# Sums of squares in the second input projection: one float32 product replaced by two rounded ones

## The chip, the cores and the metric

The kernel runs on one core of a Trainium2 chip. The metric is the device time of one execution in microseconds, the median of several runs.

## The reference, cut to what matters

The program is a two-layer network on 512 tokens of width 1024 (attention, gated feed-forward layers, a short convolution), followed by a second, hybrid mixer. The change lies in the second mixer's differential attention, where queries and keys are normed over 64 features and rotated:

```python
def rms_norm_2(x, w, eps=EPS):
    x = x.astype(jnp.float32)
    return x * lax.rsqrt(jnp.mean(x * x, axis=-1, keepdims=True) + eps) * w.astype(jnp.float32)
...
    proj = jnp.einsum("bsd,de->bse", hn, w_in.astype(f32))
...
    q_b = apply_rope(rms_norm_2(q_b.reshape(b, s, DIFF_HEADS, 2, DIFF_D), q_norm_w), cos, sin)
    k_b = apply_rope(rms_norm_2(k_b.reshape(b, s, DIFF_HEADS, 2, DIFF_D), k_norm_w), cos, sin)
```

`q_b` and `k_b` are 512 features each. In the kernel they are eight chunks of 128 features (two groups of 64) by 512 tokens.

## The kernel before, in words

All dense layers work on weight tiles of 1024 x 128. A tile is loaded as part of a panel of 256 columns (two tiles, 1 MB) by SyncE. ScalarE rounds it to a high part (`split_hi`, line 434), VectorE forms the low part as weights minus high part (`split_lo`, line 441), and TensorE multiplies: for each of eight chunks of the inner dimension three products, high by high, high by low and low by high (`dense_tile`, line 464), into a PSUM pair that alternates between tiles. High and low parts are of the rounded type (float32r). VectorE then evicts the tile, scaled per token.

The second input projection is one such sequence, `T_QB` to `T_OUT2`. Its tiles are numbered from 0 here. Tiles 0 to 7 give q_b and k_b, and tile r is chunk r of them. The order of work is written out by hand, one list per engine, all with one turn per tile:

- TensorE (`in2_pe`, from line 1606): the 24 products of tile t; then, for tiles 1 to 8, the sums of squares of the chunk before (`dif_sums_pe`, line 1903). The sums are a product with `pair`, a 128 x 128 table of ones in two blocks of 64, which gives every feature the sum over its group. It has had two float32 operands, `pair` and `d_sq`.
- ScalarE (`in2_act`, 1635): the high part of the weights of tile t + 2; `dif_raw_act` of chunk t (square, line 1891; copy scaled by the norm's weight, line 1892, which signals `raw`); `dif_scales_act` of chunk t - 1 (Ln and Exp on the sums, lines 1909 and 1910); `dif_hi_act` of chunk t - 2 (line 1926). Before tile 0 it computes the scale per token (lines 478, 479), for which tile 0's eviction waits.
- VectorE (`in2_dve`, 1675): the eviction of tile t (line 1693 for the first eight); the low part of the weights of tile t + 2; `dif_normed_dve` of chunk t - 1 (the swapped copy by the sine, line 1916; the addition, 1919; by the scale, 1922); `dif_lo_dve` of chunk t - 2 (line 1930).
- POOL (`dif_pool`, 1932): three short memsets after `raw` of chunk 0, then per chunk the product of the scaled copy and the cosine (line 1943), as soon as `raw` is there.
- SyncE: for each pair of chunks eight swap DMAs (`dif_swap`, line 1898), four per chunk, which copy quarters of 32 partitions of the scaled copy into each other's place; then the next weight panel (line 425), all through one queue.

In `setup_pool_tables` (2769) POOL copies small tables into rounded types during the start of the program; in the stage ahead of the projection POOL squares and adds the residual (lines 494, 497) and VectorE forms `x_lo` (line 484).

`Signals.wait(engine, name, n)` waits until the named semaphore has been raised n times. In `in2_dve` the turn ends with:

```python
                if 0 <= r - 1 < KC:
                    dif_normed_dve(dve, r - 1)
                if 0 <= r - 2 < KC:
                    dif_lo_dve(dve, r - 2)
```

Of the kernel before, what the change touches and what calls it, by code (L numbers as in the profile page):

```python
# [14 lines left out]
F32 = mybir.dt.float32  # L15
F32R = mybir.dt.float32r
BF16 = mybir.dt.bfloat16
ALU = mybir.AluOpType
ACT = mybir.ActivationFunctionType
# [3 lines left out]
P = 128  # L23
KC = D // P
META = 16
SEQ = 512
# [150 lines left out]
def program(nc, io, out):  # L177

    ctx = ExitStack()
    with ctx:  # L180
# [5 lines left out]
        def at(name, offset, shape, dtype=F32):  # L186
            size = int(np.prod(shape[1:])) * (2 if dtype is BF16 else 4)
            assert base + offset + size <= end, (name, base + offset + size - end)
            place[name] = offset + size
            return nc.alloc_sbuf_tensor_at(name, shape, dtype, offset=base + offset)  # L190
# [3 lines left out]
        def take(name, shape, dtype=F32):  # L194
            size = (int(np.prod(shape[1:])) * (2 if dtype is BF16 else 4) + 31) // 32 * 32
            t = at(name, cursor[0], shape, dtype)
            cursor[0] += size
            return t
# [8 lines left out]
        raw = take("raw", [P, 2, 2304])  # L207
# [3 lines left out]
        tab = {}  # L211
        for n in ("ident", "ones", "pair", "zeros"):
            tab[n] = take("t_" + n, [P, P])
        id_r, neg_r = take("id_r", [P, P], BF16), take("neg_r", [P, P], BF16)
        id_half, tri_half = take("id_half", [P, 2, P], BF16), take("tri_half", [P, 2, P], BF16)
        scale_bc = take("scale_bc", [P, LEN])
# [9 lines left out]
        z = take("z", [P, KC, LEN])  # L226
        lat = take("lat", [P, 6, LEN])
        spare = cursor[0] + 10240
# [3 lines left out]
        q_hi = take("q_hi", [P, 2, 2, LEN], F32R)  # L232
# [21 lines left out]
        ps = ctx.enter_context(nc.psum_tensor("ps", [P, 8, 512], F32))  # L254
# [6 lines left out]
        def sems(prefix, names):  # L261
            return {n: sem(f"{prefix}_{n}") for n in names.split()}
# [3 lines left out]
        s_id, s_tab0 = sem("ident_landed"), sem("first_tables_landed")  # L266
        s_vz = sem("vec_cleared")
# [23 lines left out]
        def col(name, i=0, rows=P, row0=0):  # L291
            c = VEC_ROWS[name][0] + i
            return vec[row0:row0 + rows, c:c + 1]
# [265 lines left out]
        fv = sems("forget", "cleared min ln pos sum hi lo")  # L559
# [973 lines left out]
        def conv_dve(dve):  # L1533
# [22 lines left out]
            with dve.Fori(0, 2) as i:  # L1556
                for j in range(4):
# [23 lines left out]
        d_g, d_sq, d_rs, d_sin, d_cos = [[at(f"{n}{i}", dz_at[2 * m + i], [P, SEQ]) for i in range(2)]  # L1581
                                         for m, n in enumerate(("dif_g", "dif_sq", "dif_rs", "dif_rot_a", "dif_rot_b"))]
        rows = at("rows", off["raw"], [P, 8, SEQ])
        in2 = sems("in2", "sig taps0 taps act mul params lam")

        def qk_a(c):
# [88 lines left out]
        def in2_dve(dve):  # L1675
# [8 lines left out]
            for t in range(T_QB, T_OUT2):  # L1684
# [27 lines left out]
                    dif_normed_dve(dve, r - 1)  # L1712
                if 0 <= r - 2 < KC:
                    dif_lo_dve(dve, r - 2)
                if t == T_Z:
                    dve.wait_ge(s_tab2, 144)
                    dve.tensor_tensor(small[0:64, 31:32], small[0:64, 24:25], small[0:64, 25:26], ALU.mult)
                    dve.tensor_tensor(small[0:64, 32:33], small[0:64, 26:27], small[0:64, 27:28], ALU.mult).then_inc(in2["params"], 1)
# [96 lines left out]
        class Signals:  # L1815
# [7 lines left out]
            def wait(self, eng, what, n):  # L1823
                if n > 0:
# [4 lines left out]
        finished.update({"o_unit": (fx["added"], additions(8)), "o_two": (fx["o_done"], 8), "o_sum": (fx["inv"], 8), "o_one": (fx["meta_out"], 8), "o_sq": (fx["meta_max"], 8),  # L1829
                         "l2_sq": (fx["squares"], KC), "raw": (mq["raw"], 8), "cleared": (mq["cleared"], 11), "rot_a": (mq["sin"], 5),  # L1830
                         "rot_b": (mq["cos"], 5), "rot": (mq["roped"], 5)})
        dz = Signals("dif", "raw sums rot_a rot_b rot scales normed q_hi q_lo full max exp pv out_hi out_lo cleared "
                          "shift o_sum o_one o_two o_sq o_unit o_gated l2_sq l2_inv l2_normed", finished)
        dif_order = dif_ring()
        dif_first = {T_BA - 1: [("s", 0, 3), ("s", 0, 2)], T_BA: [("s", 0, 1), ("s", 0, 0)]}
# [49 lines left out]
        def dif_raw_act(act, n):  # L1885
            act.wait_ge(evicted, T_QB + n + 1)
            dz.wait(act, "sums", n - 1)
            dz.wait(act, "rot_b", n - 1)
            if n >= 2:
                act.wait_ge(s_swap[n % 2], 16 + 64 * (n // 2))  # L1890
            act.activation(d_sq[n % 2][:, :], z[:, n, 0:SEQ], ACT.Square)
            act.activation(d_g[n % 2][:, :], z[:, n, 0:SEQ], ACT.Copy, scale=col("q_norm_w_2" if n < 4 else "k_norm_w_2")).then_inc(dz.s["raw"], 1)

        def dif_swap(eng, n):
            dz.wait(eng, "raw", n + 1)
# [2 lines left out]
                eng.dma_start(d_sin[n % 2][32 * q:32 * q + 32, :], d_g[n % 2][32 * (q ^ 1):32 * (q ^ 1) + 32, :]).then_inc(s_swap[n % 2], 16)  # L1898

        def dif_sums_pe(pe, n):  # L1900
            dz.wait(pe, "raw", n + 1)
            dz.wait(pe, "scales", n - 1)
            pe.matmul(ps[:, 5 + 2 * (n % 2), :], tab["pair"][:, :], d_sq[n % 2][:, :], start=True, stop=True).then_inc(dz.s["sums"], 1)

        def dif_scales_act(act, n):
            dz.wait(act, "sums", n + 1)
# [21 lines left out]
        def dif_lo_dve(dve, n):  # L1928
            dz.wait(dve, "q_hi", n + 1)
            dve.tensor_tensor(fox_lo[:, n, 0:SEQ], z[:, n, 0:SEQ], fox_hi[:, n, 0:SEQ].bitcast(F32), ALU.subtract).then_inc(dz.s["q_lo"], 1)  # L1930
# [836 lines left out]
            pool.memset(v_one[:, :, :, 64:128], 1.0).then_inc(fv["cleared"], 1)  # L2767

        def setup_pool_tables(pool):
            pool.wait_ge(s_tab, 16 * 9)  # L2770
            pool.wait_ge(s_id, 16)
            pool.wait_ge(first_sum, KC - 1)
            pool.tensor_copy(id_r[:, :], tab["ident"][:, :])
            pool.tensor_copy(neg_r[:, :], neg_in[:, :])
            pool.tensor_copy(id_half[:, :, :], id_half_in[:, :, :])
            pool.tensor_copy(tri_half[:, :, :], tri_half_in[:, :, :])
            pool.tensor_copy(sel_r[:, :, :].rearrange("q a b -> q (a b)"), sel_in[:, :]).then_inc(tab_ok, 1)
# [198 lines left out]
```

## Time and profile before

| what | value |
|---|---|
| median of 3 runs | 1674.76 us (1673.95 to 1680.09) |
| the profiled execution: its time | 1672.01 us |
| the profiled execution: span of the trace | 1670.2 us |
| TensorE busy | 1644.2 us, 98% |
| VectorE busy | 875.1 us, 52% |
| ScalarE busy | 625.1 us, 37% |
| POOL busy | 168.8 us, 10% |
| granted TensorE clock | 1.0 throughout |

The span is what the trace covers of one execution; the execution's own time is 1.8 us longer. Busy times add up over stages with different limits. In the profile PE is TensorE, DVE VectorE, ACT ScalarE, SPq the queue of SyncE; "L1903" is a line of the kernel. Products on TensorE are pipelined, so their records overlap: the distance between starts tells what one costs, and the chain of waits counts it that way. The number in brackets behind a timeline row is the engine's idle time before it, with what ended it.

### The profile page before, as it was taken

To read this page: it belongs to the slowest core of one execution; us is meant where nothing else is said; L and a number is where in the kernel's file an instruction comes from. 1 tells how busy PE (TensorE), PEld (TensorE's weight loads), DVE (VectorE), ACT (ScalarE), POOL (GpSimd) and SP (SyncE) were. 2 spreads that over 40 slices of the span, in tenths; PEclk is the share of its full clock that TensorE was granted. 3 is DMA by queue.
4 is the path that set the end of the run, shared out by engine and by line. 5 is a ranking of instruction groups with operands and counts; after the bars stand their busy time and mean duration, and the time that the engine had idled before them with its cause. 6 is when DMAs were issued, how large, how long until landed. Compare 5 with 4: busy or idle time off the path is not lost.

```text
span 1670.2 us, 28296 instructions
## 1 busy us (share of the span) xinstructions
PE 1644.2 (98%) x11935; PEld 1432.8 (86%) x11935; DVE 875.1 (52%) x1124; ACT 625.1 (37%) x954; POOL 168.8 (10%) x142
## 2 busy tenths in 40 slices
PE   8999999999999999999999999999999999989998
PEld 8997777899999999999987888888887788757796
DVE  6544576464343434565656434343466747866644
ACT  5523544333231323321233314132334545576223
POOL 1002213230000000220004000000033100000200
PEclk9999999999999999999999999999999999999999
DMA  6231000132332322323223322332246666101001
GB/s 194 77 83 26 8 25 28 52 102 79 99 102 77 100 83 93 101 76 101 93 83 102 101 81 96 101 100 83 93 117 103 116 89 100 29 1 61 28 27 51
DMA packets 137604, 131.92 MB, mean 79 GB/s; under 512 B 18205, under 2 KB 131860, under 8 KB 137508
## 3 DMA queue, kind: packets, MB, share of 16 engines
q1 hardware_dynamic: 137306, 130.47, 27.9%
q8 instruction: 73, 1.20, 0.3%
q14 instruction: 23, 0.19, 0.0%
q10 hardware_dynamic: 202, 0.06, 0.0%
HBM read 126.33 MB, written 2.10 MB: 77 GB/s over the span
## 4 chain that ended last, share of the span: by engine, by line
PE 94%; DVE 3%; ACT 1%; issue 0%; SPq 0%; DMA 0%; POOL 0%; ACTq 0%; DVEq 0%
PE ps L464 74%; PE ps L2275 2%; PE ps L799 2%; PE ps L782 2%; PE ps L1168 1%; PE ps L909 1%; PE ps L2006 1%; PE ps L807 1%; PE ps L2800 1%; PE ps L2447 1%; PE ps L2426 1%; PE ps L2442 1%; PE ps L1976 1%; PE ps L1174 0%; PE ps L1211 0%; PE ps L815 0%
## 5 line engine op out<-in xcount | busy, mean ns | idle before, releaser
L434 ACT ACTIVATE w_hi<-raw 128x1024 fp32r<-128x1024 f32 (+1 forms) x227 | 239.6, 1056 | 794.1 <-PE ps L464 780.1
L464 PE MATMUL ps<-x_hi,w_hi 128*128 128x258 f32 (+4 forms) x1640 | 450.3, 327 | 0.5 <-DVE x_lo L484 0.4
L464 PE MATMUL ps<-x_lo,w_hi 128*128 128x258 f32 (+4 forms) x1640 | 444.0, 323 | 0.0
L464 PE MATMUL ps<-x_hi,w_lo 128*128 128x258 f32 (+4 forms) x1640 | 443.1, 323 | 0.0
L441 DVE TENSOR_TENSOR w_lo<-raw,w_hi 128x1024 fp32r<-128x1024 f32 (+1 forms) x227 | 295.0, 1300 | 95.9 <-ACT w_hi L434 95.9
L464 PEld LDWEIGHTS ps<-x_hi,w_hi 128*128 128x128 f32 (+2 forms) x1640 | 273.1, 188 | 31.5 <-issue 3.3
L464 PEld LDWEIGHTS ps<-x_lo,w_hi 128*128 128x128 f32 (+2 forms) x1640 | 272.1, 187 | 27.6 <-issue 2.4
L464 PEld LDWEIGHTS ps<-x_hi,w_lo 128*128 128x128 f32 (+2 forms) x1640 | 272.0, 188 | 25.6
L464 PE MATMUL ps<-a_hi,w_lo 128*128 128x258 f32 (+1 forms) x960 | 255.2, 320 | 0.0
L464 PE MATMUL ps<-a_hi,w_hi 128*128 128x258 f32 (+1 forms) x960 | 255.0, 320 | 0.0
L464 PE MATMUL ps<-a_lo,w_hi 128*128 128x258 f32 (+1 forms) x960 | 255.0, 320 | 0.0
L464 PEld LDWEIGHTS ps<-a_hi,w_hi 128*128 128x128 f32 x960 | 159.1, 189 | 14.5 <-DVE a_lo L1567 0.2
L464 PEld LDWEIGHTS ps<-a_hi,w_lo 128*128 128x128 f32 x960 | 159.5, 189 | 14.0
L464 PEld LDWEIGHTS ps<-a_lo,w_hi 128*128 128x128 f32 x960 | 159.2, 189 | 14.0
L1416 DVE TENSOR_TENSOR h<-h,ps 128x516 f32<-128x516 f32 (+1 forms) x80 | 55.2, 690 | 196.7 <-PE ps L464 196.7
L1483 DVE SCALAR_TENSOR_TENSOR tmp<-ps,scale_bc 128x516 f32<-128x516 f32 (+1 forms) x64 | 44.4, 693 | 172.5 <-PE ps L464 162.6
L494 POOL TENSOR_TENSOR acc<-h 128x516 f32<-128x516 f32 (+1 forms) x4 | 4.2, 1044 | 791.4 <-DVE h L1416 791.4
L497 POOL TENSOR_TENSOR acc<-acc,sq 128x516 f32<-128x516 f32 (+1 forms) x28 | 60.4, 2155 | 2.2
L484 DVE SCALAR_TENSOR_TENSOR x_lo<-h,vec,x_hi 128x516 fp32r<-128x516 f32 (+2 forms) x40 | 58.4, 1474 | 0.1
L1488 DVE TENSOR_TENSOR a_lo<-tmp,a_hi 128x516 fp32r<-128x516 f32 (+1 forms) x64 | 44.4, 694 | 1.0 <-ACT a_hi L1465 0.5
L1465 ACT ACTIVATE a_hi<-tmp 128x516 fp32r<-128x516 f32 (+1 forms) x64 | 40.6, 635 | 2.0
L1463 ACT ACTIVATE tmp<-tmp 128x516 f32<-128x516 f32 (+1 forms) x64 | 39.5, 617 | 1.9 <-DVE tmp L1483 1.9
(441 smaller groups left out, 1781.1 us busy)
## 6 DMA issues: line engine op xcount, KB each, us to landing
raw<-in_w_mlp_up SPq DMA_DIRECT2D x32, 1024.0 KB, 5.3
raw<-in_w_mlp_down SPq DMA_DIRECT2D x32, 1024.0 KB, 4.8
raw<-in_w_in SPq DMA_DIRECT2D x16, 1024.0 KB, 9.0
raw<-in_w_in_conv SPq DMA_DIRECT2D x12, 1024.0 KB, 5.1
raw<-in_w_in_attn SPq DMA_DIRECT2D x8, 1024.0 KB, 5.1
raw<-in_w_out_attn SPq DMA_DIRECT2D x4, 1024.0 KB, 5.9
raw<-in_w_out_conv SPq DMA_DIRECT2D x4, 1024.0 KB, 4.8
raw<-in_w_out SPq DMA_DIRECT2D x4, 1024.0 KB, 5.2
```

The lines of the kernel that those rows point to most:

```text
L434: act.activation(split_tile(w_hi, t), raw_tile(t), ACT.Copy).then_inc(w_hi_ok, 1)
L441: dve.tensor_tensor(lo, raw_tile(t), hi.bitcast(F32), ALU.subtract).then_inc(w_lo_ok, 1)
L464: ins = pe.matmul(tile_banks(t)[0:m, b, 0:c], w[:, k, :], x[:, k, x0:x0 + c], start=(k == order[0] and n == 0), stop=(k == order[-1] and n ...
L484: dve.scalar_tensor_tensor(x_lo[:, c, f:], h[:, c, f:], col(*nm.gain(c)), x_hi[:, c, f:].bitcast(F32), ALU.mult, ALU.subtract).then_inc(x_ ...
L497: pool.tensor_tensor(acc[:, f:], acc[:, f:], sq[:, f:], ALU.add).then_inc(acc_ok, 1)
L782: ins = pe.matmul(slot[0:nq, x, c0:c0 + nk], q, k, start=(n == 0), stop=(n == last))
L799: ins = pe.matmul(slot[0:nk, x, c0:c0 + nq], k, q, start=(n == 0), stop=(n == last))
L1416: dve.tensor_tensor(like(dst, width), like(dst, width), in_psum(pair_of_banks[t % 2], width), ALU.add).then_inc(evicted, 1)
L1463: act.activation(tmp[:, j % 2, 0:nm.width], tmp[:, j % 2, 0:nm.width], ACT.Square).then_inc(relu_sq, 1)
L1465: act.activation(a_hi[:, j, 0:nm.width], tmp[:, j % 2, 0:nm.width], ACT.Copy).then_inc(a_hi_ok, 1)
L1483: dve.scalar_tensor_tensor(like(tmp[:, j % 2, 0:w], w), in_psum(pair_of_banks[(t0 + j) % 2], w), 0.0, like(scale_bc[:, f:], w), ALU.max, A ...
L1488: dve.tensor_tensor(a_lo[:, j, 0:w], tmp[:, j % 2, 0:w], a_hi[:, j, 0:w].bitcast(F32), ALU.subtract).then_inc(a_lo_ok, 1)
```

## The change

The sums of squares are computed from rounded operands. `pair` is copied once into a rounded table `pair_r` by POOL during setup. For every chunk ScalarE writes the square twice, in float32 (`d_sq`) and rounded (`d_sqh`); VectorE forms the difference as the low part (`d_sql`, in the place of `d_sq`), at the end of its turn for the tile; TensorE waits for the low part and adds two products, `pair_r` by high and `pair_r` by low, in one PSUM bank. ScalarE's scaled copy, which raises `raw`, comes ahead of the squares.

```diff
--- before.py
+++ after.py
@@ -211,6 +211,7 @@
         tab = {}
         for n in ("ident", "ones", "pair", "zeros"):
             tab[n] = take("t_" + n, [P, P])
+        pair_r = take("pair_r", [P, P], F32R)
         id_r, neg_r = take("id_r", [P, P], BF16), take("neg_r", [P, P], BF16)
         id_half, tri_half = take("id_half", [P, 2, P], BF16), take("tri_half", [P, 2, P], BF16)
         scale_bc = take("scale_bc", [P, LEN])
@@ -1581,6 +1582,8 @@
         d_g, d_sq, d_rs, d_sin, d_cos = [[at(f"{n}{i}", dz_at[2 * m + i], [P, SEQ]) for i in range(2)]
                                          for m, n in enumerate(("dif_g", "dif_sq", "dif_rs", "dif_rot_a", "dif_rot_b"))]
         rows = at("rows", off["raw"], [P, 8, SEQ])
+        d_sqh = at("dif_sq_hi", spare, [P, 2, SEQ], F32R)
+        d_sql = [at(f"dif_sq_lo{i}", dz_at[2 + i], [P, SEQ], F32R) for i in range(2)]
         in2 = sems("in2", "sig taps0 taps act mul params lam")
 
         def qk_a(c):
@@ -1712,6 +1715,8 @@
                     dif_normed_dve(dve, r - 1)
                 if 0 <= r - 2 < KC:
                     dif_lo_dve(dve, r - 2)
+                if r < KC:
+                    dif_squares_dve(dve, r)
                 if t == T_Z:
                     dve.wait_ge(s_tab2, 144)
                     dve.tensor_tensor(small[0:64, 31:32], small[0:64, 24:25], small[0:64, 25:26], ALU.mult)
@@ -1829,7 +1834,8 @@
         finished.update({"o_unit": (fx["added"], additions(8)), "o_two": (fx["o_done"], 8), "o_sum": (fx["inv"], 8), "o_one": (fx["meta_out"], 8), "o_sq": (fx["meta_max"], 8),
                          "l2_sq": (fx["squares"], KC), "raw": (mq["raw"], 8), "cleared": (mq["cleared"], 11), "rot_a": (mq["sin"], 5),
                          "rot_b": (mq["cos"], 5), "rot": (mq["roped"], 5)})
-        dz = Signals("dif", "raw sums rot_a rot_b rot scales normed q_hi q_lo full max exp pv out_hi out_lo cleared "
+        finished.update({"sq_hi": (s_tab0, 48), "sq_lo": (s_vz, 1)})
+        dz = Signals("dif", "raw sq_hi sq_lo sums rot_a rot_b rot scales normed q_hi q_lo full max exp pv out_hi out_lo cleared "
                           "shift o_sum o_one o_two o_sq o_unit o_gated l2_sq l2_inv l2_normed", finished)
         dif_order = dif_ring()
         dif_first = {T_BA - 1: [("s", 0, 3), ("s", 0, 2)], T_BA: [("s", 0, 1), ("s", 0, 0)]}
@@ -1888,8 +1894,13 @@
             dz.wait(act, "rot_b", n - 1)
             if n >= 2:
                 act.wait_ge(s_swap[n % 2], 16 + 64 * (n // 2))
+            act.activation(d_g[n % 2][:, :], z[:, n, 0:SEQ], ACT.Copy, scale=col("q_norm_w_2" if n < 4 else "k_norm_w_2")).then_inc(dz.s["raw"], 1)
             act.activation(d_sq[n % 2][:, :], z[:, n, 0:SEQ], ACT.Square)
-            act.activation(d_g[n % 2][:, :], z[:, n, 0:SEQ], ACT.Copy, scale=col("q_norm_w_2" if n < 4 else "k_norm_w_2")).then_inc(dz.s["raw"], 1)
+            act.activation(d_sqh[:, n % 2, :], z[:, n, 0:SEQ], ACT.Square).then_inc(dz.s["sq_hi"], 1)
+
+        def dif_squares_dve(dve, n):
+            dz.wait(dve, "sq_hi", n + 1)
+            dve.tensor_tensor(d_sql[n % 2][:, :], d_sq[n % 2][:, :], d_sqh[:, n % 2, :].bitcast(F32), ALU.subtract).then_inc(dz.s["sq_lo"], 1)
 
         def dif_swap(eng, n):
             dz.wait(eng, "raw", n + 1)
@@ -1898,9 +1909,12 @@
                 eng.dma_start(d_sin[n % 2][32 * q:32 * q + 32, :], d_g[n % 2][32 * (q ^ 1):32 * (q ^ 1) + 32, :]).then_inc(s_swap[n % 2], 16)
 
         def dif_sums_pe(pe, n):
-            dz.wait(pe, "raw", n + 1)
+            dz.wait(pe, "sq_lo", n + 1)
             dz.wait(pe, "scales", n - 1)
-            pe.matmul(ps[:, 5 + 2 * (n % 2), :], tab["pair"][:, :], d_sq[n % 2][:, :], start=True, stop=True).then_inc(dz.s["sums"], 1)
+            if n == 0:
+                pe.wait_ge(fv["cleared"], 5)
+            pe.matmul(ps[:, 5 + 2 * (n % 2), :], pair_r[:, :], d_sqh[:, n % 2, :], start=True, stop=False)
+            pe.matmul(ps[:, 5 + 2 * (n % 2), :], pair_r[:, :], d_sql[n % 2][:, :], start=False, stop=True).then_inc(dz.s["sums"], 1)
 
         def dif_scales_act(act, n):
             dz.wait(act, "sums", n + 1)
@@ -2767,6 +2781,8 @@
             pool.memset(v_one[:, :, :, 64:128], 1.0).then_inc(fv["cleared"], 1)
 
         def setup_pool_tables(pool):
+            pool.wait_ge(s_tab0, 48)
+            pool.tensor_copy(pair_r[:, :], tab["pair"][:, :]).then_inc(fv["cleared"], 1)
             pool.wait_ge(s_tab, 16 * 9)
             pool.wait_ge(s_id, 16)
             pool.wait_ge(first_sum, KC - 1)
```

## Rows read from the trace of the kernel before

**Rows 1.** The page's head, busy times and the chain that ended last, by engine.

```profile
span 1670.2 us, 28296 instructions
...
PE 1644.2 (98%) x11935; PEld 1432.8 (86%) x11935; DVE 875.1 (52%) x1124; ACT 625.1 (37%) x954; POOL 168.8 (10%) x142
...
PE 94%; DVE 3%; ACT 1%; issue 0%; SPq 0%; DMA 0%; POOL 0%; ACTq 0%; DVEq 0%
```

**Rows 2.** Chain that ended last, in order of time: start us, us, what.

```profile
1276.15 0.86 PE ps L1903 x2
1277.01 5.56 PE ps L464 x24
...
1295.41 0.86 PE ps L1903 x2
...
1321.09 0.86 PE ps L1903 x2
```

**Rows 3.** The line of the sums: records x count, ns min/median/max.

```profile
L1903 PE MATMUL ps<-dif_sq,t_pair x16: 592/592/593, 1276.0 to 1321.4; 128*128 128x512 f32 x16
```

**Rows 4.** VectorE's timeline, turn of tile 2: start us, us, instruction, idle before.

```profile
1282.61 0.69 DVE L1693 TENSOR_TENSOR z<-ps,scale_bc 128x512 f32<-128x512 f32 x1 [0.74 <-PE ps L464]
1283.76 1.23 DVE L441 TENSOR_TENSOR w_lo<-raw,w_hi 128x1024 fp32r<-128x1024 f32 x1 [0.46 <-ACT w_hi L434]
1284.90 0.68 DVE L1916 TENSOR_TENSOR dif_rot_a<-dif_rot_a,dif_sin 128x512 f32<-128x512 f32 x1
1285.62 1.67 DVE L1919 TENSOR_TENSOR z<-dif_rot_a,dif_rot_b 128x512 f32<-128x512 f32 x1
1287.33 0.69 DVE L1922 TENSOR_TENSOR z<-z,dif_rs 128x512 f32<-128x512 f32 x1
1287.94 0.68 DVE L1930 TENSOR_TENSOR fox_lo<-z,fox_hi 128x512 fp32r<-128x512 f32 x1
1289.03 0.69 DVE L1693 TENSOR_TENSOR z<-ps,scale_bc 128x512 f32<-128x512 f32 x1 [0.41 <-PE ps L464]
```

**Rows 5.** VectorE's timeline, stage before, turn of tile 3, eviction of tile 4.

```profile
1261.38 1.77 DVE L484 SCALAR_TENSOR_TENSOR x_lo<-h,vec,x_hi 128x512 fp32r<-128x512 f32 x1
...
1294.12 0.69 DVE L1916 TENSOR_TENSOR dif_rot_a<-dif_rot_a,dif_sin 128x512 f32<-128x512 f32 x1 [2.72 <-DMA dif_rot_a<-dif_g]
...
1296.79 0.68 DVE L1693 TENSOR_TENSOR z<-ps,scale_bc 128x512 f32<-128x512 f32 x1
```

**Rows 6.** ScalarE's timeline, chunk 0 and the turn of tile 2.

```profile
1274.13 0.63 ACT L1891 ACTIVATE dif_sq<-z 128x512 f32<-128x512 f32 x1 [0.76 <-DVE z L1693]
1274.67 0.71 ACT L1892 ACTIVATE dif_g<-z,vec 128x512 f32<-128x512 f32 x1
...
1282.67 1.06 ACT L434 ACTIVATE w_hi<-raw 128x1024 fp32r<-128x1024 f32 x1 [2.98 <-PE ps L464]
1283.63 0.62 ACT L1891 ACTIVATE dif_sq<-z 128x512 f32<-128x512 f32 x1
1284.15 0.71 ACT L1892 ACTIVATE dif_g<-z,vec 128x512 f32<-128x512 f32 x1
```

**Rows 7.** POOL's timeline: setup, the stage before, products of chunks 0, 2, 3.

```profile
27.88 0.29 POOL L2773 CAST id_r<-t_ident 128x128 bf16<-128x128 f32 x1 [23.98 <-DVE acc L529]
...
1260.45 2.15 POOL L497 TENSOR_TENSOR acc<-acc,sq 128x512 f32<-128x512 f32 x1
...
1276.35 1.29 POOL L1943 TENSOR_TENSOR dif_rot_b<-dif_g,dif_cos 128x512 f32<-128x512 f32 x1
...
1284.94 1.80 POOL L1943 TENSOR_TENSOR dif_rot_b<-dif_g,dif_cos 128x512 f32<-128x512 f32 x1 [5.08 <-ACT dif_g L1892]
1291.36 1.30 POOL L1943 TENSOR_TENSOR dif_rot_b<-dif_g,dif_cos 128x512 f32<-128x512 f32 x1 [4.62 <-ACT dif_g L1892]
```

**Rows 8.** SyncE's timeline: DMAs issued, merged; x8 is two chunks' swaps.

```profile
1280.98 0.52 SPq L425 DMA_DIRECT2D raw<-in_w_in  x1
1284.89 8.84 SPq L1898 DMA_DIRECT2D dif_rot_a<-dif_g  x8
```

## The prediction

> **What bounds the kernel now.** I read the page's head first: TensorE is busy for 98% of the span and makes 94% of the chain that ended last [rows 1]. A microsecond on TensorE is therefore a microsecond of the kernel, and work elsewhere costs only if TensorE waits for it. Next the chain around the change: each weight tile of the second input projection is 24 products in 5.56 us, which is 0.232 us for a product of 512 columns, and behind each of the first eight tiles after tile 0 stands the sum of squares with 0.86 us, back to back from 1276.15 to 1321.09 [rows 2]. So the period of a tile is 5.56 + 0.86 = 6.42 us, with no wait in it. The 0.86 us is one float32 product, shown as two records of 592 ns that overlap in the pipeline [rows 3].
>
> Then the other engines in one period. I number tiles from the start of this projection (tile 2 is done at 1282.57). VectorE's turn for tile 2 is the eviction, the low part of weights, the three steps of the rotation of chunk 1, and the low part of chunk 0: from 1282.61 to 1287.94 + 0.68 = 1288.62, and the next eviction starts at 1289.03, 0.41 us after it [rows 4]. VectorE is thus almost full here, though its share of the whole span is 52% [rows 1]. One of its steps lasts 1.67 us instead of 0.69: the rotation's addition, which ends 0.55 us after POOL's product (1284.94 + 1.80 = 1286.74; 1285.62 + 1.67 = 1287.29) [rows 4, 7]. It doesn't need that product, which is of chunk 2, so the two share something. The same picture stands in the stage before: VectorE's x_lo ends at 1263.15, 0.55 us after POOL's addition at 1262.60 [rows 5, 7]. Where VectorE was idle, POOL's product took 1.30 us; where it was asked for just after VectorE's step had begun, 1.80 [rows 7].
>
> Last, SyncE: the swaps of chunks 2 and 3 stand in the same queue behind the weight panel issued at 1280.98; chunk 2's swap is issued from 1284.89, but VectorE waits for it until 1294.12, for 2.72 us [rows 5, 8]. That turn (tile 3) ends so late that the eviction of tile 4 starts at 1296.79, though tile 4 was done at 1295.41 [rows 2, 5]. It costs nothing now, because an eviction has most of a tile's time to spare.
>
> **The change, part by part.** (1) The product: one float32 product of 0.86 us becomes two of rounded operands. Their form is that of the weight tiles' products, 0.232 us each [rows 2]. Gain 8 x (0.86 - 0.464) = 3.17 us, and the period TensorE could keep is 6.03 us.
>
> (2) ScalarE: a third operation per chunk. Square takes 0.62, the scaled copy 0.71, and in a row they start 0.52 to 0.54 us apart [rows 6]. ScalarE stands idle for 2.98 us ahead of tile 2's weights [rows 6], which hides 8 x 0.5; without that cover it would be 4 us. The high square is ready at 1284.15 + 0.5 + 0.6, some 1285.3, over 2 us ahead of VectorE's need.
>
> (3) The low part of the square on VectorE, last in its turn, and TensorE now waits for it ahead of the sums. Its form is that of the low part of a chunk: it adds 0.61 us to the turn (1287.94 - 1287.33 is the step between two such operations) [rows 4]. The turn of tile 2 then ends at 1288.62 + 0.61 = 1289.23, with 0.05 for the signal 1289.28, that is 6.71 us after tile 2 was done. TensorE has 0.46 + 5.56 = 6.02 us of work until it asks, so it waits 0.7 us. Behind the wait stands the whole next tile; behind the low part on VectorE stands the next eviction. That eviction starts 0.6 us late, but then the 0.46 us that VectorE stands between eviction and low weights, waiting for ScalarE (1283.76 [rows 4]), is gone, so the next turn takes 6.16 and TensorE waits about 0.1. Waits of 0.7 and 0.1 take turns: 0.4 per tile, just what (1) gives per tile.
>
> (4) The copy ahead of the squares: the raw signal comes 0.52 us earlier. The eight groups of four swap DMAs on SyncE and POOL's product start earlier by that. For POOL it changes what it meets: the copy starts when ScalarE has ended the high weights, together with VectorE's low weights (1283.63 and 1283.76), and ends 0.71 later, in the middle of them (1.23 long) [rows 4, 6]. The low weights are then in progress, POOL's product waits for their end and holds up the rotation's first step instead of its second. I take the same 1 us of delay as now. If POOL got out of the way it would be 0; if both of VectorE's steps were held up, 2 us per tile.
> The Trainium skill (SBUF — State Buffer, section "SBUF: two separate sides") says that VectorE, for instructions with two SBUF inputs, and GpSimd take a shared port pair as an exclusive lock for a whole instruction, whoever starts first. By that rule moving the copy ahead brings VectorE nothing, since the product is serialized with it wherever it lands; the trace agrees in the 0.55 us. Without such a lock the sum below would be -0.4 instead of +2.3.
>
> (5) Tile 0. Its eviction waits for the scale, so ScalarE squares only at 1274.13 and TensorE asks for the sums at 1276.15 [rows 2, 6]. With copy, square, high square the last ends at 1274.13 + 0.62 + 0.54 + 0.61 = 1275.9. POOL starts its product 0.55 earlier than 1276.35 [rows 7], at 1275.8, just ahead of VectorE's low part, which by the pattern ends 0.55 after 1275.8 + 1.29: 1277.6. Wait 1.5 us; if VectorE came first, 0.5.
>
> (6) Tile 3 and the late swap. Panel and swaps are issued 0.55 us earlier, so chunk 2's swap lands near 1293.6. The rotation, two low parts and the new one follow: 0.72 + 0.73 + 0.61 + 0.60 + 0.69 = 3.35, plus what the turn before has shifted the queue (1.1 us by the waits of (5) and (3), less the 0.4 per tile gained). It is ready at about 1298.1, where TensorE asks at 1296.6: wait 1.5 us. The bounds are 1 lower or higher, by when the panel lands. The other two late swaps fall into turns that are already late and add nothing.
>
> (7) Setup: one cast more on POOL ahead of the tables. POOL stands idle there for 24.0 us [rows 7], so nothing; its neighbour of the same size takes 0.29 us, which is the upper end if it held up VectorE. TensorE's wait for it is over a thousand microseconds late.
>
> Sum, with the turns written out tile by tile: waits of 1.6 (tile 0), 0, 0.8, 1.5 (tile 3), 0.05, 0.7, 0.05, 0.7 = 5.4 us, against the gain of 3.17: **+2.3 us**. After tile 8 TensorE is again ahead of everything and hands the shift on to the end unchanged. The profiled execution took 1672.01 us for a span of 1670.2, so the sum gives 1674.3 there; the median of the runs is 1674.76, so 1677.0.
>
> **The rivals.**
> A. TensorE never waits: VectorE's new operation fits, since it stands idle 0.41 us there and 2.72 us for the swap. Then -3.2 us, 1671.6. Against it: 6.62 us of work in a turn of 6.02.
> B. POOL's product delays VectorE less than now once it starts earlier. Then only tile 0 (0.5) and the late swap of tile 3 (2.3) make TensorE wait: -0.4 us, 1674.4. For it: where the product meets no VectorE work it costs nothing (tile 3, 1291.36) [rows 7].
> C. Slower than forecast: VectorE's low weights are stretched as well, because the product now asks for memory in their middle, and the rotation behind them too. A step of 1.0 us more per turn makes the turn 7.2 us, and worked through the tiles it gives +5.4 us, 1680.2. It decides from the point where the copy ends before the low weights do, which is in every tile. For it: in this trace such a stretch of an operation always comes from POOL. Against it: a VectorE step already begun was not stretched (0.68 at 1284.90) [rows 4].
> D. The two rounded products are no cheaper than the one in float32, so the change doesn't do what it says: +5 to +6 us, 1680. Against it is every weight tile.
> The rule of the Trainium skill named above speaks against B.
>
> **How the numbers follow.** Forecast 0.52, A 0.12, B 0.20, C 0.12, D 0.01, and 0.03 for something outside this stage. All named cases lie within 0.5% (8.4 us, about what a measurement of this kernel can tell from no change): 1666.4 to 1683.1. Only the case outside can leave it, in either direction, and C with a doubled price. Faster 0.02, same 0.95, slower 0.03. The range takes in A at 1671.6 and C at 1680.2, plus a little for a median of few runs: 1671.3 to 1681.
>
> **What would show it.** Right: the sums at 0.46 us in the chain; waits of TensorE for the low square, in total about 5 us, the longest behind tiles 1 and 4, the rest in turns of 0.7 and under 0.1; POOL's product starting in the middle of the low weights, and the rotation's first step at about 1.7 us with the addition at 0.7. Wrong: no wait of TensorE for the low square (A), both steps of the rotation near 0.7 us (B), low weights above 1.3 us in each turn (C), sums above 0.8 us (D), or a difference that appears outside 1274 to 1325 us.

## The result, and the profile after

| | before | changed |
|---|---|---|
| median of 20 runs each | 1674.20 us | 1677.42 us |
| ratio | | 1.0021, 95% interval 1.0012 to 1.0031 |
| the profiled execution | 1672.01 us | 1677.78 us |
| granted TensorE clock, mean of the profiled execution | 1.000 | 0.998 |
| stage: statistics product to first transpose of the values | 56.40 us | 59.48 us |

The changed kernel is slower by 0.21% (2.0 to 5.2 us by the interval). 1677.0 was forecast. The change doesn't reach the 0.5% that the chances go by.

Two profiled executions can't be subtracted here without care. The changed one lies 0.44 us behind within its first 25 us (a start-up DMA landed later), and loses another 1.6 us between 270 and 305 us, a stretch in which one window of 10 us (280 to 290) has a granted clock of 0.86. It loses 0.6 us more from 1555 to 1560 us, where the granted clock is 0.66. Both are means over a part at 2.4 GHz and a part at the lower level, 1.2 GHz. The kernel before has 1.00 in both places, though its TensorE had stood idle as long just ahead of them (1.0 of 5 us and 1.3 of 5 us in both kernels). No instruction of the change runs there.

The prediction named a difference outside 1274 to 1325 us as a sign of being wrong. These 2.6 us are such a difference, but they go with the clock and the start-up of single executions and not with the change. So I compare the **stage**: the distance on TensorE from the start of the statistics product in tile 1 to the first transpose of the values behind tile 9. It grew by 3.08 us.

The chain of waits of the changed kernel, by time (start, us, what). Before, it held nothing but TensorE here [rows 2].

```profile
1278.00 1.72 DVE dif_sq_lo L1903
...
1279.76 0.50 PE ps L1916
1280.27 0.23 PE ps L1917
1280.50 5.59 PE ps L465 x24
...
1291.08 5.55 DMA dif_rot_a<-dif_g
...
1299.47 0.61 DVE dif_sq_lo L1903
...
1300.13 0.50 PE ps L1916
...
1300.85 5.57 PE ps L465 x24
...
1310.57 0.70 DVE z L1933
...
1311.29 0.69 DVE z L1936
1311.98 0.60 DVE fox_lo L1944
1312.59 0.61 DVE dif_sq_lo L1903
...
1313.24 0.50 PE ps L1916
```

Now the end of VectorE's turn stands in the chain ahead of the sums in several tiles: the low square (L1903), and in front of it the rest of the turn. Behind tile 4 even a swap DMA does (1291.08).

The groups of waits of the same stretch (engine, line, what it waited for: us in total, times, longest):

```profile
PEld ps L1916 <- DVE dif_sq_lo L1903: 7.4, 7, 2.0
...
PE ps L1916 <- DVE dif_sq_lo L1903: 4.7, 5, 1.5
...
DVE dif_rot_a L1930 <- DMA dif_rot_a<-dif_g: 2.1, 1, 2.1
```

From the starts of its products I read what TensorE needs between the last of a tile's 24 products and the first of the next tile's; I call it the **gap**. (PEld in the rows is TensorE's weight load.) Before, it is 0.86 us eight times. In order of the chunks it is now 2.27, 0.46, 1.54, 1.64, 0.55, 1.45, 0.55, 1.44 us, in sum 9.90 against 6.88: the 3.0 us of the stage.

VectorE's turn for tile 2 in the changed kernel (start, us, instruction, idle time before it), which answers to [rows 4]:

```profile
1286.12 0.69 DVE L1696 TENSOR_TENSOR z<-ps,scale_bc 128x512 f32<-128x512 f32 x1 [0.91 <-PE ps L465]
1287.27 1.22 DVE L442 TENSOR_TENSOR w_lo<-raw,w_hi 128x1024 fp32r<-128x1024 f32 x1 [0.46 <-ACT w_hi L435]
1288.41 1.78 DVE L1930 TENSOR_TENSOR dif_rot_a<-dif_rot_a,dif_sin 128x512 f32<-128x512 f32 x1
1290.23 0.69 DVE L1933 TENSOR_TENSOR z<-dif_rot_a,dif_rot_b 128x512 f32<-128x512 f32 x1
1290.96 0.69 DVE L1936 TENSOR_TENSOR z<-z,dif_rs 128x512 f32<-128x512 f32 x1
1291.57 0.68 DVE L1944 TENSOR_TENSOR fox_lo<-z,fox_hi 128x512 fp32r<-128x512 f32 x1
1292.17 0.69 DVE L1903 TENSOR_TENSOR dif_sq_lo<-dif_sq,dif_sq_hi 128x512 fp32r<-128x512 f32 x1
1292.77 0.68 DVE L1696 TENSOR_TENSOR z<-ps,scale_bc 128x512 f32<-128x512 f32 x1
```

It lasts 6.65 us to the next eviction, where TensorE has 6.02 us of work. VectorE's steps alone, back to back, would take 6.1 us of it; the rest comes from the wait ahead of the low weights. The long step has moved from the addition (L1919 before, L1933 now) to the sine product (L1916 before, L1930 now). POOL's timeline answers to [rows 7]:

```profile
1277.89 1.27 POOL L1957 TENSOR_TENSOR dif_rot_b<-dif_g,dif_cos 128x512 f32<-128x512 f32 x1
...
1287.93 1.72 POOL L1957 TENSOR_TENSOR dif_rot_b<-dif_g,dif_cos 128x512 f32<-128x512 f32 x1 [5.33 <-ACT dif_g L1897]
```

The product now starts inside the low weights (1287.27 to 1288.49), ends at 1289.65, and the sine product ends at 1290.19, 0.54 us behind it.

### The profile page after: what moved, and what is told of

Same layout as the page of the kernel before. It is cut to its first block, busy times and chain, and to the rows that moved or that the text cites. A ratio compares the mean times of both kernels' runs of the same rounds, so it can differ in the third digit from the quotient of the medians.

```text
span 1676.0 us, 28314 instructions
## 1 busy us (share of the span) xinstructions
PE 1644.8 (98%) x11935; PEld 1433.1 (86%) x11935; DVE 882.7 (53%) x1132; ACT 629.7 (38%) x962; POOL 168.9 (10%) x143
## 4 chain that ended last, share of the span: by engine, by line
PE 92%; DVE 4%; ACT 2%; DMA 1%; issue 1%; SPq 1%; ACTq 0%; DVEq 0%
PE ps L465 72%; PE ps L2289 2%; PE ps L800 2%; PE ps L783 2%; PE ps L1169 1%; PE ps L910 1%; PE ps L2020 1%; PE ps L2816 1%; PE ps L808 1%; PE ps L2461 1%; PE ps L2440 1%; PE ps L2456 1%; PE ps L1990 1%; PE ps L1175 0%; PE ps L1212 0%
```

## The experiments

"Before" below is always the kernel before, run on the same chip in the same rounds. The ratio to it comes with its 95% interval. The interval is about 2 us wide to either side, so steps of less than that are read from the stage of each kernel's profile. A stage is read from one execution: two profiles of the changed kernel gave 59.48 and 60.05 us, and the 0.6 us between them are in one gap, that of chunk 3, by when a swap landed.

| kernel | ratio to before | stage, us | gaps, chunk 0 to 7, us |
|---|---|---|---|
| before | | 56.40 | 0.86 each |
| changed | 1.0021 (1.0012 to 1.0031) | 59.48 | 2.27 0.46 1.54 1.64 0.55 1.45 0.55 1.44 |
| copy_first | 1.0002 (0.9988 to 1.0016) | 56.39 | 0.86 each |
| high_twice | 0.9985 (0.9972 to 0.9999) | 53.31 | 0.54, then 0.46 to 0.47 |
| low_early | 0.9991 (0.9979 to 1.0003) | 55.03 | 2.28, then 0.47 each |
| pool_writes_only | 1.0018 (1.0006 to 1.0030) | 56.99 | 1.26 0.47 0.82 2.34 0.47 0.82 0.46 0.81 |
| squares_first | 1.0025 (1.0011 to 1.0039) | 59.50 | 0.62 1.44 0.46 3.61 0.46 1.42 0.46 1.48 |
| no_swap | 1.0005 (0.9991 to 1.0019) | 58.35 | 2.26 0.46 1.54 0.52 1.46 0.52 1.50 0.50 |
| low_early_squares_first | 0.9999 (0.9986 to 1.0013) | 54.47 | 0.62 0.47 0.47 0.47 1.15 0.57 0.59 0.57 |
| chunk_low_twice | 1.0033 (1.0021 to 1.0046) | 61.33 | 2.25 0.46 2.14 1.76 1.13 1.48 1.13 1.47 |
| low_early_chunk0_squares_first | 1.0003 (0.9993 to 1.0014) | 54.04 | 0.65 0.47 0.47 0.47 0.89 0.53 0.51 0.51 |
| low_early_product_first | 0.9995 (0.9983 to 1.0007) | 54.31 | 1.55, then 0.47 each |
| change_again | 1.0016 (1.0002 to 1.0029) | 60.05 | 2.28 0.46 1.53 2.22 0.52 1.48 0.53 1.45 |

### copy_first: only the order on ScalarE

```diff
-            act.activation(d_sq[n % 2][:, :], z[:, n, 0:SEQ], ACT.Square)
             act.activation(d_g[n % 2][:, :], z[:, n, 0:SEQ], ACT.Copy, scale=...).then_inc(dz.s["raw"], 1)
+            act.activation(d_sq[n % 2][:, :], z[:, n, 0:SEQ], ACT.Square).then_inc(dz.s["sq_hi"], 1)
...
-            dz.wait(pe, "raw", n + 1)
+            dz.wait(pe, "sq_hi", n + 1)
```

> The kernel before with the scaled copy ahead of the one square, and nothing else of the change. Theory (shared memory port of VectorE and POOL, whoever comes first holds it): POOL's product now starts in the middle of the low weights and holds up the rotation's first step (about 1.7 to 1.8 us) where it held up the addition; the turn stays 6.0 us, TensorE still never waits except perhaps 0 to 0.1 us for chunk 0: time within 0.5 us of before, and the stretch from the statistics product to the values' transposes stays 56.4 us. Rival (moving the copy is what costs): this kernel alone shows +1 us or more and TensorE waits for squares behind tile 1 and tile 4.

The gaps stay at 0.86, the stage at 56.39. VectorE's turn for tile 2 (columns as above):

```profile
1285.32 1.78 DVE L1916 TENSOR_TENSOR dif_rot_a<-dif_rot_a,dif_sin 128x512 f32<-128x512 f32 x1
1287.14 0.69 DVE L1919 TENSOR_TENSOR z<-dif_rot_a,dif_rot_b 128x512 f32<-128x512 f32 x1
```

The sine product has become the long step and the addition the short one, as the changed order alone would have it. The turn's work is 0.13 us longer (6.14 us against 6.01), which the idle time ahead of the next eviction takes up. The rival, by which the moved copy is what costs, falls.

### high_twice: no work for VectorE

```diff
-                if r < KC:
-                    dif_squares_dve(dve, r)
...
-            pe.matmul(ps[:, 5 + 2 * (n % 2), :], pair_r[:, :], d_sql[n % 2][:, :], start=False, stop=True)...
+            pe.matmul(ps[:, 5 + 2 * (n % 2), :], pair_r[:, :], d_sqh[:, n % 2, :], start=False, stop=True)...
```

TensorE waits for the high square here.

> The change without VectorE's low part: TensorE multiplies the high square twice, so the low part is left out of the sums. Theory: the two products cost 0.46 us in place of 0.86 and TensorE waits for nothing, so the stage is 3.2 us shorter than before (53.2 us) and the time about 3 us below before. Rival (rounded products don't come cheaper, or ScalarE's third operation is what holds up TensorE): the stage is no shorter than 56 us.

The stage is 53.31 us, 3.09 below before, and this is the only kernel whose interval lies wholly below 1. The gain of the two products is all there as long as nothing is awaited, and ScalarE's third operation costs no more than the 0.07 us by which the first gap is longer.

### low_early: the low part elsewhere in the turn

```diff
                 if t + 2 < T_OUT2:
                     split_lo(dve, t + 2)
+                if r < KC:
+                    dif_squares_dve(dve, r)
                 if 0 <= r - 1 < KC:
                     dif_normed_dve(dve, r - 1)
                 if 0 <= r - 2 < KC:
                     dif_lo_dve(dve, r - 2)
-                if r < KC:
-                    dif_squares_dve(dve, r)
```

> The change with VectorE's low part moved from the end of its turn to right behind the low weights, ahead of the rotation. Theory (TensorE waits only because of where the low part stands in the turn): VectorE is still full at 6.6 us per turn and falls behind by some 0.6 us per tile, but nobody waits for the end of the turn, so TensorE waits only behind tile 1 (about 1.5 us); the stage is 3.2 - 1.5 = 1.7 us shorter than before, 54.7 us. Rival (VectorE's total work is the bound wherever the low part stands): the waits only change their name, TensorE waits for low weights, and the stage stays near the 59.5 us of the changed kernel.

55.03 us: 4.45 below the changed kernel and 1.4 below before. VectorE does the same work and has even more waiting in it (0.70 us in most turns for ScalarE's high square), yet TensorE waits once:

```profile
DVE dif_sq_lo L1903 <- ACT dif_sq_hi L1899: 5.3, 8, 0.7
...
PE ps L1916 <- DVE dif_sq_lo L1903: 1.5, 1, 1.5
```

From tile 3 on VectorE stays behind TensorE, and but for the turn with the late swap its turns start 6.10 us apart:

```profile
1298.73 0.68 DVE L1696 TENSOR_TENSOR z<-ps,scale_bc 128x512 f32<-128x512 f32 x1
...
1304.83 0.68 DVE L1696 TENSOR_TENSOR z<-ps,scale_bc 128x512 f32<-128x512 f32 x1
```

So the 6.6 us per turn that the theory named were wrong: 0.5 us of them were the idle time ahead of the low weights, which a late turn doesn't have, and VectorE falls behind by 0.1 us per tile, not 0.6. In the changed kernel a tile of the same stretch takes 6.56 us on average (the sums at 1300.13 and 1313.24 are two tiles apart), more than VectorE's work or TensorE's. What makes it slow is that TensorE asks for the result of VectorE's last step and VectorE then finds itself ahead and waits in its turn. The rival, by which the total work is the bound, falls; a VectorE with clearly more work per turn than TensorE's 6.02 us wasn't tried with the low part early. Chunk 0 keeps its 2.28: there the low square starts late because ScalarE starts late, wherever it stands in the turn. VectorE's timeline shows what it then meets:

```profile
1277.50 1.71 DVE L1903 TENSOR_TENSOR dif_sq_lo<-dif_sq,dif_sq_hi 128x512 fp32r<-128x512 f32 x1 [0.70 <-ACT dif_sq_hi L1899]
```

POOL's product of chunk 0 had started at 1277.40.

### pool_writes_only: POOL reads nothing

```diff
-                pool.tensor_tensor(d_cos[n % 2][:, :], d_g[n % 2][:, :], dif_cos[:, :], ALU.mult)...
+                pool.memset(d_cos[n % 2][:, :], 0.5)...
```

> The change with POOL's product replaced by a constant written to the same place, so the rotation leaves out the cosine. POOL then reads nothing from memory. Theory (the product holds up VectorE by 1.0 us per turn): the rotation's first step falls from 1.78 to 0.7 us, the turn from 6.6 to 5.6, and only chunk 0 (0.5 us) and the late swap of chunk 2 (about 2 us) make TensorE wait; the stage is 2.5 to 3 us shorter than in the changed kernel, some 56.5 us. Rival (VectorE's step is long for another reason, such as waiting for ScalarE's copy): it stays at 1.78 and the stage at 59.5.

The stage is 56.99 us, 2.5 shorter than in the changed kernel. Both rotation steps are short; POOL's write of 0.53 us now ends inside the low weights (columns as above):

```profile
1285.38 0.68 DVE L1930 TENSOR_TENSOR dif_rot_a<-dif_rot_a,dif_sin 128x512 f32<-128x512 f32 x1
1286.09 0.69 DVE L1933 TENSOR_TENSOR z<-dif_rot_a,dif_rot_b 128x512 f32<-128x512 f32 x1
1287.20 0.69 DVE L1936 TENSOR_TENSOR z<-z,dif_rs 128x512 f32<-128x512 f32 x1 [0.41 <-ACT dif_rs L1924]
...
1297.54 1.21 DVE L442 TENSOR_TENSOR w_lo<-raw,w_hi 128x1024 fp32r<-128x1024 f32 x1
1298.68 0.68 DVE L1930 TENSOR_TENSOR dif_rot_a<-dif_rot_a,dif_sin 128x512 f32<-128x512 f32 x1
1299.39 0.69 DVE L1933 TENSOR_TENSOR z<-dif_rot_a,dif_rot_b 128x512 f32<-128x512 f32 x1
1300.77 0.69 DVE L1936 TENSOR_TENSOR z<-z,dif_rs 128x512 f32<-128x512 f32 x1 [0.68 <-ACT dif_rs L1924]
```

So 1.1 us of the step of 1.78 is POOL's. That it is POOL's reading, and not only its longer stay, shows at chunk 0, where the write runs while the low square does and the low square isn't stretched:

```profile
1275.86 0.53 POOL L1957 MEMSET dif_rot_b<- 128x512 f32 x1
...
1275.98 0.69 DVE L1903 TENSOR_TENSOR dif_sq_lo<-dif_sq,dif_sq_hi 128x512 fp32r<-128x512 f32 x1 [0.70 <-ACT dif_sq_hi L1899]
```

Not foreseen is the idle time of 0.41 and 0.68 us ahead of L1936. Once VectorE is quicker it waits for ScalarE's Exp (L1924). The chain of waits shows that ScalarE isn't waiting for the sums there; it works without a pause from the high weights on, for which it had waited until TensorE ended the tile, and its third operation of the chunk, the high square, stands in that chain:

```profile
1305.65 0.52 ACT dif_sq_hi L1899
1306.18 0.58 ACT dif_rs L1923
...
1306.78 0.64 ACT dif_rs L1924
...
1307.52 0.69 DVE z L1936
```

Gaps of 0.82 stand where that holds. The ratio of this kernel is worse than its stage; nine of its twelve executions had a mean clock of 0.997 or below. At equal clock (the fit below) it is 1.5 +- 0.6 us above before, where the stage has 0.6 us, so the clock accounts for most of the difference and not for all.

### squares_first: both squares ahead of the copy

```diff
-            act.activation(d_g[n % 2][:, :], z[:, n, 0:SEQ], ACT.Copy, scale=...).then_inc(dz.s["raw"], 1)
             act.activation(d_sq[n % 2][:, :], z[:, n, 0:SEQ], ACT.Square)
             act.activation(d_sqh[:, n % 2, :], z[:, n, 0:SEQ], ACT.Square).then_inc(dz.s["sq_hi"], 1)
+            act.activation(d_g[n % 2][:, :], z[:, n, 0:SEQ], ACT.Copy, scale=...).then_inc(dz.s["raw"], 1)
```

> The changed kernel with both squares ahead of the scaled copy again. Theory (chunk 0's low square waits for POOL's product, chunk 2's late swap sets the wait behind tile 4): the low square of chunk 0 now comes before the product, so TensorE waits at most 0.1 us behind tile 1 in place of 1.5; all swaps are issued 1.05 us later, so the wait behind tile 4 stays or grows by up to 1 us; the rest keeps its pattern. Stage 58 to 58.7 us against 59.5. Rival (the order on ScalarE doesn't matter): 59.5.

Half of it came as expected: the gap of chunk 0 falls from 2.27 to 0.62. But that of chunk 2's swap (fourth in the row) grows by 2 us, not by at most one, so the stage is 59.50, no better. VectorE waits for the swap until 1297.44, 3.08 us, against 2.14 us in the changed kernel:

```profile
1297.44 0.69 DVE L1930 TENSOR_TENSOR dif_rot_a<-dif_rot_a,dif_sin 128x512 f32<-128x512 f32 x1 [3.08 <-DMA dif_rot_a<-dif_g]
```

This isn't a swap that lands 2 us later: VectorE's step behind it starts 23.9 us after the start of the stage, against 23.7 us in the changed kernel. TensorE was there 1.75 us sooner, since its first three gaps took 2.52 us and not 4.27. What it gains ahead of the swap it waits for at the swap. So the order on ScalarE decides where the wait stands, and the stage hardly changes.

### no_swap: no swap DMAs

```diff
-            for q in range(4):
-                eng.dma_start(d_sin[n % 2][32 * q:32 * q + 32, :], d_g[n % 2][...]).then_inc(s_swap[n % 2], 16)
...
-            dve.tensor_tensor(d_sin[n % 2][:, :], d_sin[n % 2][:, :], dif_sin[:, :], ALU.mult)...
+            dve.tensor_tensor(d_sin[n % 2][:, :], d_g[n % 2][:, :], dif_sin[:, :], ALU.mult)...
```

ScalarE waits for the sine product before it writes the copy again.

> The changed kernel without the swap DMAs: the sine product reads the scaled copy itself, so the rotation leaves out the exchange of halves. Theory (the swap of chunk 2 behind the weight panel makes the wait behind tile 4): VectorE never waits for a DMA, the gap behind tile 4 falls to 0.5 to 0.6 us and the alternation of 0.5 and 1.45 goes on behind it; stage 58 to 58.6 us. Rival (VectorE would be late there anyway): the gap behind tile 4 stays at 1.6 us.

The gap behind tile 4 is 0.52 us, the stage 58.35. The late swap is worth 1.1 us. It can be worth more: in change_again the same gap is 2.22 us, as the swap landed with VectorE's step at 1296.68, while TensorE was 0.6 us earlier than in the first profile.

### chunk_low_twice: one more operation per turn

```diff
+            dve.tensor_tensor((acc, sq)[n % 2][:, 0:SEQ], z[:, n, 0:SEQ], fox_hi[:, n, 0:SEQ].bitcast(F32), ALU.subtract)
             dve.tensor_tensor(fox_lo[:, n, 0:SEQ], z[:, n, 0:SEQ], fox_hi[:, n, 0:SEQ].bitcast(F32), ALU.subtract)...
```

> The changed kernel with one more VectorE operation of 0.61 us per turn from tile 2 on: the low part of the chunk is also written to a spare place. Theory (VectorE's turn with TensorE's wait at its end sets the period): each of the six turns from tile 2 on that end in a low square is 0.6 us longer and all of it reaches TensorE, but for the up to 0.46 us that the turn behind a late one gets back: stage 59.5 + 2.5 to 3.6 us, 62 to 63.1. Rival (TensorE's waits have another cause, such as ScalarE or the signal): 59.5 to 60.

61.33 us: 1.85 more, below the 2.5 to 3.6 expected. Of the six turns, three pass on 0.58 to 0.60 us (gaps 1.54 to 2.14, 0.55 to 1.13 twice), and three next to nothing (1.64 to 1.76, 1.45 to 1.48, 1.44 to 1.47). The direction is the theory's; its size shows how much a late turn gets back: per pair of turns the changed kernel has idle time of 0.28 us ahead of an eviction and 0.46 us ahead of the low weights, and here only 0.25 us ahead of the low weights is left.

### Three versions meant to beat both

The first has the edits of low_early and of squares_first together.

> Low part right behind the low weights, and both squares ahead of the copy: what should beat both kernels. Theory: the low square of chunk 0 is done before POOL's product starts, and no low square is awaited at any tile; every gap is 0.46 to 0.54 us, the stage 53.3 us, the time 3 us below before (ratio 0.998). Rival: the later copy makes the swaps so late that VectorE falls behind by more than a tile and TensorE waits for an eviction or for low weights; then the stage is over 55 us.

The gaps of the first four chunks are as expected, but from chunk 4 on they are 1.15, 0.57, 0.59 and 0.57, and the stage is 54.47, not 53.3. VectorE waits 3.84 us for chunk 2's swap and evicts tile 4 only at 1298.56, 3.8 us behind its end. What TensorE then waits for is again the low square (0.41 us behind tile 5), which stands early in a turn that starts late; neither the theory nor the rival, which had over 55 us, is right:

```profile
1291.36 0.69 DVE L1903 TENSOR_TENSOR dif_sq_lo<-dif_sq,dif_sq_hi 128x512 fp32r<-128x512 f32 x1
1295.89 0.69 DVE L1930 TENSOR_TENSOR dif_rot_a<-dif_rot_a,dif_sin 128x512 f32<-128x512 f32 x1 [3.84 <-DMA dif_rot_a<-dif_g]
```

The second is low_early with the squares ahead of the copy for chunk 0 alone:

```diff
-            act.activation(d_g[n % 2][:, :], z[:, n, 0:SEQ], ACT.Copy, scale=...).then_inc(dz.s["raw"], 1)
+            def copy():
+                act.activation(d_g[n % 2][:, :], z[:, n, 0:SEQ], ACT.Copy, scale=...).then_inc(dz.s["raw"], 1)
+            if n:
+                copy()
             act.activation(d_sq[n % 2][:, :], z[:, n, 0:SEQ], ACT.Square)
             act.activation(d_sqh[:, n % 2, :], z[:, n, 0:SEQ], ACT.Square).then_inc(dz.s["sq_hi"], 1)
+            if n == 0:
+                copy()
```

> Low part right behind the low weights; for chunk 0 alone both squares ahead of the copy, for all others the copy first. Theory (what is left in low_early is the collision of chunk 0's low square with POOL's product, what went wrong in low_early_squares_first are the late swaps and copies of all other chunks): the gap behind tile 1 falls from 2.28 to about 0.6 us, the others stay at 0.47; stage 53.3 to 53.5 us, time 3 us below before. Rival: the swaps of chunks 0 and 1, issued 1.05 us later, delay the panel and chunk 2's swap so far that gaps from tile 5 on exceed 0.5 us; stage 54 us or more.

54.04 us. The gap of chunk 0 is 0.65, as the theory had it; for the rest the rival was right: the gaps from chunk 4 on are above 0.5 (0.89 the first) and the stage is over 54.

The third is low_early with POOL's three memsets behind the product of chunk 0:

```diff
-            pool.memset(v_sum[:, :, :, P:P + 1], 1.0).then_inc(dz.s["cleared"], 1)
...
             for n in range(KC):
                 dz.wait(pool, "raw", n + 1)
                 dz.wait(pool, "rot", n - 1)
                 pool.tensor_tensor(d_cos[n % 2][:, :], d_g[n % 2][:, :], dif_cos[:, :], ALU.mult).then_inc(dz.s["rot_b"], 1)
+                if n == 0:
+                    pool.memset(v_sum[:, :, :, P:P + 1], 1.0).then_inc(dz.s["cleared"], 1)
...
```

> Low part right behind the low weights, the copy first everywhere, and POOL's product of chunk 0 ahead of the three memsets. Theory: the product starts 0.9 us earlier, right after the copy, ends about 1.3 to 1.4 us later, and holds up chunk 0's low square until 0.55 us behind its end, 0.9 us earlier than in low_early; gap behind tile 1 about 1.4 us in place of 2.28, the rest 0.47; stage 54.1 us. Rival (the low square is late because ScalarE's high square is late): the gap stays at 2.2 us.

54.31 us, close to the 54.1 expected, and all gaps but the first at 0.47. The low square of chunk 0 is the third of these rows of its chain:

```profile
1276.65 0.52 ACT dif_sq L1898
1277.18 0.53 ACT dif_sq_hi L1899
...
1277.73 1.01 DVE dif_sq_lo L1903
...
1278.78 0.51 PE ps L1916
1279.29 0.23 PE ps L1917
```

Beside them ran the changed kernel once more, without an edit.

> The changed kernel once more, beside the two others on the same chip: stage 59.5 us, ratio 1.002 as found, against 0.998 for the first of the three if its theory holds.

Its ratio is 1.0016 and its stage 60.05 us. Each of the four kernels with the early low part has a stage 1.4 to 2.4 us shorter than before and 4.5 to 5.4 shorter than the changed kernel. Against the changed kernel they have the lower ratios (0.9991, 0.9999, 1.0003 and 0.9995 against 1.0021 and 1.0016), though their intervals overlap that of change_again; the fit below sets all four clearly apart from it. That they beat the kernel before is shown for the stage; for the whole time all four intervals hold 1. The executions of one kernel spread over more than 4 us with their mean granted clock, which lies between 0.994 and 1.000 over all kernels. A fit of the 249 executions that have a clock on record (one level per kernel, one slope for the clock) gives 1.4 us per 0.001 of clock and, at equal clock, +3.6 +- 0.4 us for the changed kernel, -3.1 +- 0.6 for high_twice, and -0.9, -1.6, -1.6 and -1.3, each +- 0.65, for the four, in the order of the table. For these kernels that agrees with the stages to within about 0.8 us.

## Why the prediction was right

**The sum.** +2.3 us was forecast against before; measured are +3.2 by the medians and +3.1 for the stage. That 1677.4 came so near to 1677.0 is in part luck, for the forecast started from a median of 1674.76 and the one measured beside the change is 1674.20. (The sum also took 1.6 and 0.8 us where its steps (5) and (3) have 1.5 and 0.7, and 5.4 - 3.17 is 2.2.) The forecast's gaps, 0.46 plus its waits, were 2.06, 0.46, 1.26, 1.96, 0.51, 1.16, 0.51, 1.16 (sum 9.1). Measured: 2.27, 0.46, 1.54, 1.64, 0.55, 1.45, 0.55, 1.44 (sum 9.9).

**Steps (1) and (2), the products and ScalarE: right.** A gap without a wait is 0.46 to 0.47 us, and high_twice returns the whole 3.1 us. ScalarE's third operation hides in the changed kernel, but for chunk 0, where step (5) counted it; it would not hide if VectorE were quicker, as pool_writes_only shows.

**Step (3), the last place in the turn: right, and shown.** The turn is 6.65 us for 6.02 of TensorE's work, and waits of more and less take turns. low_early separates the cause: same operations, other place, 4.45 us less. What I mis-sized is the longer of the two waits. The gap is 1.45 where 0.46 + 0.7 = 1.16 was forecast, since the first product behind a wait takes 0.50 us, not 0.23. TensorE's timeline of the changed kernel:

```profile
1279.76 0.50 PE L1916 MATMUL ps<-dif_sq_hi,pair_r 128*128 128x512 f32 x1 [1.54 <-DVE dif_sq_lo L1903]
1280.11 0.39 PE L1917 MATMUL ps<-dif_sq_lo,pair_r 128*128 128x512 f32 x1
1280.34 0.39 PE L465 MATMUL ps<-x_hi,w_hi 128*128 128x512 f32 x1
```

The chain puts 0.50 on the first product, 0.27 more than on one in a row. Of this 0.12 us stand between the starts: the second product starts 0.35 us behind the first, against 0.23 us for the next. That goes with the weights, which aren't loaded ahead, as the loads wait for the low square too (the row `PEld ps L1916` above: 7 times, 7.4 us); no run has the one without the other. The other 0.15 us or so are the length of a record (0.39 us) over the distance of two starts (0.23), which shows only behind a pause. Five gaps carry these 0.27 us, 1.3 us in sum. This is the term that the sum lacked. The waits themselves were less than forecast, 4.7 us in sum against 5.4, mostly at the late swap (0.9 against 1.5), and hid part of it.

**Step (4), the moved copy: right.** copy_first gives 0 us of stage (at equal clock +0.5 +- 0.6 us), and the held-up step has moved as described. The Trainium skill (SBUF — State Buffer, "SBUF: two separate sides") states the exclusive lock of the port pair, and that VectorE's operations with two SBUF inputs meet it only against a GpSimd operation that reads SBUF. The traces here agree with both: 0.54 us between the ends with the product, no stretch of a low square that a memset overlaps (0.69 us at 1275.98 in pool_writes_only).

**Step (5), chunk 0: right.** 1.5 us of wait were expected, from the collision with POOL's product. The row of waits has 1.5 as its longest. The collision is shown by three runs: squares_first avoids it (0.62), pool_writes_only takes the reader away (1.26, which leaves the wait of 0.5 us that the step named for this case), low_early_product_first moves it forward (1.55).

**Step (6), the late swap: mechanism right.** The gap is 1.64 us where 1.96 was forecast, and it moves from profile to profile (2.22 in change_again), within the 1 us either way that was allowed. no_swap takes it away. By squares_first it isn't a term of its own: it grows by what TensorE saves ahead of it.

**Step (7), the setup: right, within 0.05 us.** The cast ran at 15.85 us for 0.41 us while POOL was idle, beside VectorE's eight x_lo operations. These take 5.52 us in the two kernels without the cast (before, copy_first) and 5.55 or 5.56 us in all with it. The 0.44 us by which the profiled execution was later there stem from a DMA that landed before the cast; in low_early, which has the cast too, the x_lo start 0.14 us earlier than before.

**The rivals.** A fell with the first wait behind tile 1. B needed POOL's product to delay VectorE less once it starts earlier, and in copy_first it delays the sine product to 1.78 us. C needed stretched low weights, and they stayed at 1.21 to 1.23 us in the changed kernel, where each had begun before the product or ran clear of it. Where the product begins first they are stretched: in squares_first POOL's starts at 1279.47, and the low weights of 1279.95 take 1.89 us. D fell with high_twice.

## What to carry to other kernels

Ask of a new wait where in the producer's list the awaited step stands. An engine that is full but whose results have a tile's time to spare costs nothing; put a result that the bounding engine wants at once at the end of its list, and its whole load becomes visible. Here 0.4 us per tile was gained on TensorE and more than that lost to a step of 0.6 us, while the same step four operations earlier keeps 1.4 of the 3.1 us gained.

When the order on one engine is changed, check what each of its consumers then collides with: the copy ahead of the squares helped the swaps, and sent POOL's product of chunk 0 into the low square that TensorE was waiting for.

## What the runs showed of the hardware that I had not expected

A product that had to wait for a semaphore cost 0.27 us more than one that had not (0.50 against 0.23), and its weight load had waited with it. VectorE and POOL take turns at what they share: a POOL product that had asked during the low weights got its turn ahead of VectorE's next operation, which was then 1.1 us longer (1.78 against 0.68): so in the changed kernel, copy_first, high_twice, no_swap and chunk_low_twice, and not where POOL only wrote. The stage before the change behaved the same way [rows 5, 7]. And a mean granted clock lower by 0.001 goes with 1.4 us, so that a few tenths of a per cent of time between single executions say nothing about an edit of this size.
